# A three-part transformer kernel on one core: the residual stream kept transposed

## The reference, cut to what matters

```
rms_norm(x, g):  x * rsqrt(mean(x*x, over features) + 1e-6) * g

for layer in 0, 1:
    x = x + 0.5 * (silu(h @ Wgate) * (h @ Wup)) @ Wdown      h = rms_norm(x, ffn1_norm)     d_ff 2816
    x = x + mixer(rms_norm(x, mix_norm)) @ w_out             layer 0: two attentions, layer 1: dilated attention
    x = x + cross_attention(rms_norm(x, xa_norm), memory of 256 rows) @ w_o
    x = x + 0.5 * ffn(rms_norm(x, ffn2_norm))
third block:
    h = rms_norm(x, norm_mix_pre)
    q, k, v, index scores, recurrence, gates = h @ w_in      (5192 + 1024 columns, in parts)
    y = gate_a * (recurrence @ w_rnn_out) + gate_b * (top-k attention @ w_att_out)
    x = x + rms_norm(y @ w_o, norm_mix_post)
    f = ffn(rms_norm(x, norm_ffn_pre))
    out = x + rms_norm(f @ w_ffn_down, norm_ffn_post)
```

## Time and profile before

| | |
|---|---|
| median of 3 runs | 3215.26 us |
| the profiled execution | 3217.18 us, of it the traced span 3215.4 us |
| granted TensorE clock | 0.995 |
| TensorE matmul busy | 3142.1 us, 98% of the span, 14548 instructions |
| VectorE, ScalarE, GpSimd busy | 1410.1, 1193.3 and 251.9 us |
| DMA | 291.45 MB, mean 91 GB/s |
| transposes of xn (line 97) | 352 |

### The profile page before, as it was taken

One profiled execution on the slowest core, in us unless ns is written; L12 is line 12 of the kernel. 1 busy time (PEld: TensorE's weight loads), 2 busy tenths in 40 slices (PEclk: granted clock), 3 DMA queues, 4 the chain that ended last, 5 costly groups with the idle time before them and its releaser, 6 DMA issues.

```text
span 3215.4 us, 37017 instructions
## 1 busy us (share of the span) xinstructions
PE 3142.1 (98%) x14548; PEld 2530.2 (79%) x14548; DVE 1410.1 (44%) x2212; ACT 1193.3 (37%) x2007; POOL 251.9 (8%) x517
## 2 busy tenths in 40 slices
PE   8999999999999999999999999999999999989998
PEld 6888886777888888888867878888887776778887
DVE  3332348654333243323465644332335776543322
ACT  3322237543332133222455533322325636432321
POOL 1000014110000000000310100000042100010000
PEclk9999999999999999999999999999999999999999
DMA  4332231422333223322322412333232231223331
GB/s 142 92 103 94 92 99 34 132 72 79 99 92 104 93 91 92 105 93 91 92 93 74 149 48 91 99 92 100 82 92 73 79 105 34 86 79 99 98 97 67
DMA packets 212607, 291.45 MB, mean 91 GB/s; under 512 B 12849, under 2 KB 137009, under 8 KB 212305
## 3 DMA queue, kind: packets, MB, share of 16 engines
q1 hardware_dynamic: 209792, 279.59, 28.0%
q0 software_dynamic: 2640, 9.50, 0.9%
HBM read 286.94 MB, written 2.10 MB: 90 GB/s over the span
## 4 chain that ended last, share of the span: by engine, by line
PE 90%; ACT 4%; DVE 3%; POOL 2%; issue 1%; DMA 0%; POOLq 0%; DVEq 0%; ACTq 0%
PE ps L94 86%; PE ps L97 3%; ACT L100 0%; POOL evQ L142 0%; POOL stat L103 0%; ACT ocPb L100 0%; ACT sxPb L100 0%; ACT xn L100 0%; ACT wh L100 0%; DVE s_ri L115 0%; POOL s_ri L103 0%; ACT hTh L100 0%; POOL evPb L142 0%; DVE hTl L109 0%; DVE xn L106 0%
## 5 line engine op out<-in xcount | busy, mean ns | idle before, releaser
L103 DVE TENSOR_TENSOR wl<-raw,wh 128x1024 fp32r<-128x1024 f32 (+1 forms) x530 | 640.6, 1216 | 1166.2 <-ACT wh L100 1161.1
L100 ACT ACTIVATE wh<-raw 128x1024 fp32r<-128x1024 f32 (+1 forms) x530 | 551.8, 1051 | 1258.9 <-PE ps L94 1205.9
L94 PE MATMUL ps<-hTh,wh 128*128 128x512 f32 x2144 | 841.0, 392 | 8.5 <-DVE wl L103 4.5
L94 PE MATMUL ps<-hTh,wl 128*128 128x512 f32 x2144 | 838.0, 391 | 0.0
L94 PE MATMUL ps<-hTl,wh 128*128 128x512 f32 x2144 | 837.8, 391 | 0.0
L94 PEld LDWEIGHTS ps<-hTh,wh 128*128 128x128 f32 x2144 | 403.1, 188 | 100.3 <-DVE wl L103 6.5
L94 PEld LDWEIGHTS ps<-hTh,wl 128*128 128x128 f32 x2144 | 403.0, 188 | 84.9 <-issue 2.5
L94 PEld LDWEIGHTS ps<-hTl,wh 128*128 128x128 f32 x2144 | 403.2, 188 | 84.6 <-issue 3.4
L94 PE MATMUL ps<-wh,hTh 128*128 128x512 f32 (+2 forms) x832 | 321.5, 386 | 3.5 <-DVE hTl L109 2.6
L94 PE MATMUL ps<-wl,hTh 128*128 128x512 f32 (+2 forms) x832 | 316.6, 381 | 0.0
L94 PE MATMUL ps<-wh,hTl 128*128 128x512 f32 (+2 forms) x832 | 316.5, 380 | 0.0
(11 more groups left out here) (366 smaller groups left out, 3929.1 us busy)
## 6 DMA issues: line engine op xcount, KB each, us to landing
raw<-in_ffn_w_gu SPq DMA_DIRECT2D x352, 256.0 KB, 3.1
raw<-in_ffn_w_down SPq DMA_DIRECT2D x88, 512.0 KB, 3.5
raw<-in_xa_w_kv SPq DMA_DIRECT2D x32, 512.0 KB, 3.9
raw<-in_w_in SPq DMA_DIRECT2D x28, 512.0 KB, 3.7
raw<-in_od_w_in SPq DMA_DIRECT2D x24, 512.0 KB, 3.6
raw<-in_w_ffn_gate SPq DMA_DIRECT2D x44, 256.0 KB, 2.9
raw<-in_w_ffn_up SPq DMA_DIRECT2D x44, 256.0 KB, 3.1
raw<-in_w_ffn_down SPq DMA_DIRECT2D x22, 512.0 KB, 3.8
```

The costliest lines, as they stand in the source:

```text
L94: return self.made(lambda e: e.matmul(*a, **k))
L100: return self.made(lambda e: e.activation(*a, **k))
L103: return self.made(lambda e: e.tensor_tensor(*a, **k))
```

## The change

x is kept as `xT`, 8 tiles of 128 features x 512 tokens. The products that add to x (f1d, out, xo, f2d, wo) take form A. `hTh` and `hTl` are written from xT and the gain, without the rate, tile by tile as soon as a tile of x is complete; where the buffer is free (all but after xo) the first four tiles are written between the two groups of the product before. The squares are summed over tiles by GpSimd, 7 additions of 128x512, and over partitions by TensorE: four matmuls with a vector of ones (`pe_sums`). The rate of each token as a column is `rc`; where it is needed along the free axis, GpSimd scales an identity matrix by it and TensorE multiplies it by ones (`pe_spread`), and ScalarE copies the result to R. Results of form B are multiplied by the column where they are read, results of form A by R. For rnn, ya and gb the tiles of h are written once more, with R (`dve_again`). For the last product x is transposed back while f3d runs (`pe_back`). At the start x is transposed as loaded. `pool_recurrence` now comes before the start's rate on GpSimd.

```
-        G.append(rows(f"f1d{l}", T["ffn1_w_down"][l], KF, [512, 512], "f"))
+        G.append(rows(f"f1d{l}", T["ffn1_w_down"][l], KF, [512, 512], "f", "A"))
...
+    def act_square(act, N, src, c):
+        act.wait_ge(x_ready, (src, c))
...
+        act.activation(sq[c % 2], xT[:, c, :], AF.Square).then_inc(squared, (N, c))
+    def act_upper(act, N, src, c, gone):
+        act.wait_ge(x_ready, (src, c))
+        act.wait_ge(w_used, gone)
+        act_hi(act, xT[:, c, :], hT(N), c, slice(0, S), None, norm_gain[N][:, c:c + 1])
+    def dve_lower(dve, N, c):
+        dve_lo(dve, xT[:, c, :], hT(N), c, slice(0, S), norm_gain[N][:, c:c + 1])
+    def pool_sums(pool, N, upto=KD):
...
+            ins = pool.tensor_tensor(total, sq[0] if c == 1 else total, sq[c % 2], ALU.add).then_inc(step, (N, "sum", c))
+    def pe_sums(pe, N, b, parts, gone=()):
...
+                ins = pe.matmul(bank[b][:, t:t + 1], part[:, t * P:(t + 1) * P], ones[:, 0:1], start=n == 0,
+                                stop=n == len(parts) - 1)
+    def dve_means(dve, N, b):
+        dve.wait_ge(summed, ("sums", N))
+        dve.tensor_scalar(rc[:, 0:4], bank[b][:, 0:4], 1.0 / D, EPS, ALU.mult, ALU.add).then_inc(step, (N, "mean")).also(
+    def pool_power(pool, N):
...
+        pool.tensor_tensor(rc[:, 4:8], rc[:, 0:4], half[:, 0:4], ALU.pow).then_inc(rated, N)
+    def pe_spread(pe, N, b):
...
+        pe.matmul(bank[b][:, :], ones[:, :], spread, start=True, stop=True).then_inc(summed, ("R", N)).also(xn_gone, (N, 1))
+    def pe_rates(pe, N, g, kp):
+        if (g, kp) == (0, 2) and N != "f1u0":
+            pe_sums(pe, N, rate_bank(N), [(total, step, (N, "sum", KD - 1))], (1,) if N in no_spread else ())
+        if (g, kp) == (0, 3) and N not in no_spread:
+            pe_spread(pe, N, rate_bank(N))
...
     def dve_add(dve, name, scale, N=None):
         def evict(g):
+            lower = N is not None and (g or N in h_before)
+            for j in range(4):
+                c = 4 * g + j
+                dve.wait_ge(summed, (name, g, j))
+                dve.wait_ge(x_ready, (dve.x_last[c], c))
+                dve.scalar_tensor_tensor(xT[:, c, :], bank[home[name, g] + j][:, :], scale, xT[:, c, :], ALU.mult,
+                                         ALU.add).then_inc(x_ready, (name, c)).also(drained, (name, g, j))
+                dve.x_last[c] = name
+                if lower and j:
+                    dve_lower(dve, N, c - 1)
...
+    def dve_mix(dve, g):
...
+            for c in range(KD):
+                dve.wait_ge(step, ("mix", c))
+                ins = dve.tensor_tensor(GB[:, c, :], GB[:, c, :], bank[b][:, :], ALU.mult).then_inc(step, ("mixed", c))
...
+                dve.tensor_tensor(xT[:, c, :], xT[:, c, :], GB[:, c, :], ALU.add).then_inc(x_ready, ("wo", c))
...
+                if c:
+                    dve_lower(dve, "f3u", c - 1)
```

More of the change, by code:

```diff
@@ L516, in dve_lo @@
         return ins.then_inc(lo_done, (A.key, k))
-    stat_order = ["f1u0", "in0", "mem0", "xa0a", "xa0b", "f2u0", "f1u1", "in1", "mem1", "xa1a", "xa1b", "f2u1", "idx",
-                  "wo", "f3u", "f3d"]
+    stat_order = ["f1u0", "mem0", "mem1", "f3d"]
     stat_before = dict(zip(stat_order[1:], stat_order))
[L522 to L526, removed]
-        else:
-            e.wait_ge(x_ready, (src, t))
@@ L579, in act_norm_hi @@
-    def act_norm_hi(act, N, gain):
-        for c in chunk_order(N, 0):
-            act.wait_ge(turned, (N, c))
-            act_hi(act, bank[c][:, :], hT(N), c, slice(0, S), h_before.get(N), gain[:, c:c + 1])
-    def dve_norm_lo(dve, N, gain):
-        for c in chunk_order(N, 0):
-            dve.wait_ge(turned, (N, c))
-            dve_lo(dve, bank[c][:, :], hT(N), c, slice(0, S), gain[:, c:c + 1]).also(drained, ("norm", N, c))
-    xn_order = ["f1u0", "in0", "in0:0", "in0:1", "mem0", "xa0a", "xa0b", "kv0:2", "kv0:3", "xq0:0", "xq0:1", "f2u0", "f1u1",
-                "in1", "in1:0", "in1:1", "in1:2", "in1:3", "mem1", "xa1a", "xa1b", "kv1:2", "kv1:3", "xq1:0", "xq1:1",
-                "f2u1", "idx", "ix", "ya:1", "ya:3", "wo", "f3u", "f3d"]
+    norm_gain = {"f1u0": par("ffn1_norm0"), "in0": par("mix_norm0"), "f2u0": par("ffn2_norm0"), "f1u1": par("ffn1_norm1"),
+                 "in1": par("mix_norm1"), "f2u1": par("ffn2_norm1"), "idx": par("norm_mix_pre"), "f3u": par("norm_ffn_pre"),
+                 "xa0": par("xa_norm0"), "xa1": par("xa_norm1")}
@@ new lines, in program, with rate_bank @@
+    h_before = {"in0": "f1u0", "f1u1": "f2u0", "in1": "f1u1", "idx": "f2u1", "f3u": "yb"}
+    no_spread = ("xa0", "xa1", "in1")
+    def rate_bank(N):
+        return 4 - home[N, 0] + 3
+    def act_square(act, N, src, c):
+        act.wait_ge(x_ready, (src, c))
+        if c >= 2:
+            act.wait_ge(step, (N, "sum", max(c - 2, 1)))
+        else:
+            xn_wait(act, N, 0)
+        act.activation(sq[c % 2], xT[:, c, :], AF.Square).then_inc(squared, (N, c))
[3 more added lines that the diff above has]
+        act_hi(act, xT[:, c, :], hT(N), c, slice(0, S), None, norm_gain[N][:, c:c + 1])
@@ L593, in program, with pool_start @@
+    def pool_start(pool):
+        pool_power(pool, "f1u0")
+        spread_out(pool, "f1u0", range(NT))
+    xn_order = ["f1u0", "in0", "in0:0", "in0:1", "xa0", "kv0:2", "kv0:3", "xq0:0", "xq0:1", "f2u0", "f1u1", "in1", "in1:0", "in1:1",
+                "in1:2", "in1:3", "xa1", "kv1:2", "kv1:3", "xq1:0", "xq1:1", "f2u1", "idx", "ix", "ya:1", "ya:3", "wo",
+                "f3u", "f3d"]
     xn_before = dict(zip(xn_order[1:], xn_order))
@@ L1226, in act_post, with act_back @@
+    def act_back(act, g, kp):
+        if g == 0 and kp in (1, 2, 4, 5):
+            t = (1, 2, 4, 5).index(kp)
+            act.wait_ge(w_used, last_chunk("f3u"))
+            for u in range(2):
+                act.wait_ge(turned, ("back", t, u))
+                act.activation(x_back[:, t, 512 * u:512 * u + 512], bank[back_bank(2 * (t % 2) + u)][:, :], AF.Copy).then_inc(
+                    put, ("back", t)).also(drained, ("back", t, u))
+    def act_post(act):
         for t in range(NT):
@@ L2085, in side @@
                 pe_gates(pe, g - 1)
-        pe_gemm(pe, "rnn", {"h": hT("idx")}, side)
+        pe_gemm(pe, "rnn", {"h": hT("idx2")}, side)
     def act_rnn_side(act, g, kp):
```

674 lines of the change are left out of this document (394 added, 280 removed).

## The result

The changed kernel takes 3222.08 us (median of 17 runs, 3219.96 to 3224.00), the kernel before 3216.4 (17 runs, 3214.97 to 3217.42); the ratio is 1.0019 with an interval of 1.0012 to 1.0027. I had forecast 3195. The profiled execution has a span of 3220.4 us against 3215.4 and a granted clock of 0.991 against 0.995, so 4.9 us are to be explained by the two traces, and 25.1 between forecast and result (the sum said -20.2).

A forecast was written before the change was run, and what follows sets the result against it. TensorE's list, busy for 98% of the span, was taken as the bound. -42.4 removed, +16.8 added, +2.0 waits and +3.4 from wo to f3u gave -20.2 us: 3195 us, own range 3187 to 3203.

The forecast's parts named there:

- Six pauses and the transposes: TensorE's six pauses at norms go, 34.8 us; so do xq's transposes inside kv0 and kv1, 7.0 us.
- the new work on TensorE: Sums 6.3, spreading of rates 6.0, transposing x back 3.5, going between kinds of matmul 1.0: 16.8 us added.
- the sums: Sums over partitions on TensorE at nine places, four float32 one-column matmuls each, 0.7 us apiece: 6.3 us (4.5 to 8.1).
- rival (c): Pauses at six boundaries reach the length where the clock falls; waits of 3 us each give 3223 us; chance 0.07.
- The change of form is therefore free in itself: Products on TensorE: a matmul takes 0.227 us in form A or B alike, so changing form costs nothing.
- a period of 361 from f2u0 to f1u1: Sign of success: first matmul of f2u0 to first of f1u1 takes 361 us, not 365.
- The start: Before the third chunk: the 8.8 us coefficient chain stays but begins earlier, gaining 0.6 us (1.4 gained to 0.5 lost).
- hidden: GpSimd's seven additions per norm, 1.04 to 1.3 us each, end before TensorE asks for the sum, 16.3 us later.
- wo to f3u: Between wo's end and f3u: a loss of 21.5 us against 18.1, 3.4 longer (3 shorter to 8 longer).
- The lock: From wo to f3u, GpSimd's seven additions delay VectorE's loop by 0.55 us each, 4 us (0 to 7).
- The clock behind it: After f3u's pause before its third chunk, the lowered clock costs 1.7 us, as after the start's pause.
- the waits at idx, rnn and after xo: Late matrix at idx, late third-chunk splits at rnn and after xo, 0.5 us put on each; together 2.0 us.

The follow-up runs named there:

- g1: Changed kernel with its stages' memory moved to base 127104: 3211.7 us (0.9986).
- g2: Changed kernel with its stages' memory moved to base 126848: 3211.5 us (0.9985).
- h1: g1 with GpSimd making the start's rates ahead of the coefficients, not behind them: 3208.8 us (0.9974).
- h2: g1 with in0's R copied out of PSUM by VectorE, not by ScalarE: 3211.6 us (0.9984).
- e4: Changed kernel with stages' memory at 126720 and six of GpSimd's seven additions for xq0, xq1 and f3u cut to 8 columns: 3220.5 us (1.0015).
- h3: Kernel before with chunks 2 and 3 of f1u0 split ahead of the coefficients: 3210.9 us (0.9983).
- e2: Kernel before with only its stages' memory moved up by 64 bytes, to 126144: 3235.6 us (1.0062).
- g3: Kernel before with every buffer (h, weights, stages) moved up together by 64 bytes: 3216.4 us (0.9999).

## Why the prediction was wrong

What the change takes out and puts in on TensorE was right; what it does to the rest was not seen. Six pauses and the transposes are worth 41.6 us (41.8 forecast), and the new work on TensorE costs 16.8, as forecast (the sums 7.3 with the switching in it, where I had 6.3 and 1.0). The waits that rival (c) foresaw did not come: TensorE waits for `wl` at none of the six boundaries, and nowhere for `total`; that the time came out at its 3223 is chance. Five steps failed, in order of size.

1. The pace of the products, a term that I put at nothing. "The change of form is therefore free in itself" is true as it stands: in g1 and g2 form A steps by 226.7. The failed step is what I drew from it, that the 12,336 matmuls then take as long as before. The pace depends on where the two operands lie, and the change moved every stage's memory. This costs 11.2 by the traces (10.6 in the products named above), 10.4 by the runs (changed against g1). The sign stood in the trace of before: wo's matmuls step by 0.2334, as shown above, where the products around them step by 0.227 to 0.228. I never asked why. The sign that I had named, a period of 361 from f2u0 to f1u1, came out at 362.1, and the missing 1.2 is f2d0's pace.
2. The start, 5.3 off. I had written above that `pool_recurrence` comes before the rate, and followed the chain only to its beginning. The power and the scalings (3.4 us, whose length I had, 1.2 + 2.4) stand behind it, in the chain. h1 gives back 2.9 of them. Another 1.7 is that the coefficients begin 1.1 later, and not 0.6 earlier, behind VectorE's four copies of x.
3. in0, 4.7 off, not in my sum at all. I costed the copy of R at nothing, without asking what it stands ahead of on ScalarE and how soon TensorE wants that. The trace shows the evictions 5.2 us and the transposes 5.6 us later; h2, which moved the copy, did not settle how much of it is the copy.
4. kv0 and kv1, 3.1. I priced GpSimd's additions against VectorE only in f3u. Where I called them hidden I counted when the sum is asked for, and not what the additions do to VectorE's splits in the meantime. With six of the seven cut to 8 columns (e4) each kv is 1.65 shorter.
5. wo to f3u, 2.6. The lock was priced rightly (3.5 by e4, 4 forecast). VectorE's loop began at E + 7.5 and not 6.2: ten matmuls of the sum took 2.4 us behind the last square, at a granted clock of 1.00, where I had 1.8, and the spreading 2.05, at 0.50, where I had 1.4. So the third chunk was 1.3 late. The clock behind it cost 3.0 and not 1.7. The length of the pause doesn't explain it: 8.4 us here cost 3.0 and 8.2 us at the start of the same execution 1.8. So the price of one pause of the earlier trace rows could not be carried over; what sets it the runs don't show. The windows behind both pauses, then those of the sum and of the spreading:

```profile
37.50:41.50 4.00, 4.00 (x10) 3.18 (x11) 3.34 (x3) 1.41 (x2) 0.00 (x0) 0.55 0.65 173
2851.00:2857.00 6.00, 6.00 (x14) 4.74 (x15) 3.32 (x3) 1.39 (x2) 0.00 (x0) 0.50 0.76 230
```

```profile
2821.00:2822.00 1.00, 1.00 (x11) 1.00 (x10) 0.00 (x0) 0.00 (x0) 0.00 (x0) 1.00 0.00 0
...
2825.00:2826.00 1.00, 1.00 (x2) 0.00 (x0) 0.00 (x0) 0.00 (x0) 0.00 (x0) 0.50 0.08 16
```

That these five all have one sign is no accident: the sum was made of what the change takes out and puts in on TensorE, and each of them is, at least in part, something that the new instructions or the new tiles do to the rest. Only the waits at idx, rnn and after xo came out shorter, by 1.7.

## What to carry to other kernels

Before saying that a change leaves the matmuls alone, compute us per matmul for every stage, in both kernels, and look up where the operands lie: a constant added below a pool of buffers moves them all. Each instruction that is added is priced not only by its own length but by what stands behind it in that engine's list, and by the instructions of other engines that it holds up while it runs. A wait that comes from splits standing behind other work can be cheap to remove: two chunks split ahead at two places gave 17 us. And a gain found on the way is tried in the kernel before too, as in h3, where 6 of these 17 turned out not to belong to the change.

## What the runs showed of the hardware

- A matmul of 128x512 in fp32r steps by 226.7 ns at full clock where the starts of its stationary and its moving operand differ by a multiple of 256 bytes in a partition. With a distance of 64 bytes it is 233.3 with the stage's tile stationary and 228.9 with it moving; with 128 bytes 232.4 and 233.3; with 32 bytes 233.3 (s_Y, moving). In wo of the kernel before s_Zh lies at 32 and s_Zl at 0, and the mean is 233.4 too; in e2, with 32 and 64, it is 231.1, so the distance alone does not give the size of the loss. The address itself has no part in it (g3), nor have other engines or DMA (f3d from 3191.5 to 3203). The Trainium skill ("SBUF — State Buffer", who interferes with whom) gives TensorE one read port for the moving operand and an independent one for the loads, and says that it never waits on anyone; by that the distance of the two would not matter, and here it costs 1 to 3%. Why it does the runs don't show.
- VectorE's instructions with two inputs from SBUF and GpSimd's additions exclude each other: in VectorE 0.69 us became 1.40 and 1.23 became 2.31, and GpSimd's 1.29 became 1.78. A VectorE product with one input in PSUM kept its 0.68.
- Behind pauses of TensorE of 8.2 and 8.4 us in one execution the granted clock was 0.55 (37.5 to 41.5) and 0.50 (2851 to 2857), and cost 1.8 and 3.0 us. In work that is the same in two kernels it can be low in one execution and full in the next (g1 0.72, g2 1.00, from 1856 to 1862).
- A float32 matmul with one column takes 0.10 us a record, 0.81 for the eight (from the start of the last matmul before them to the start of the next, less one step), and 0.12 a record in wo's sum (20 in 2.39 us, clock 1.00). The spreading takes 0.86, and 2.05 at half clock.
